# Output projection and FFN of a diffusion block on Trainium2: eight weight slots taken by row tile, and norms per row tile

## What is computed

```python
y = merged @ w_out
h_state = x + g1 * rms_norm(y, norm_mix_post)
h = rms_norm(h_state, norm_ffn_pre) * (1.0 + sc2) + sh2
y = (silu(h @ ffn_w_gate) * (h @ ffn_w_up)) @ ffn_w_down
out = h_state + g2 * rms_norm(y, norm_ffn_post)
```

## Time and profile before

| | us |
|---|---|
| median of 3 runs | 1792.96 |
| lowest, highest | 1792.02, 1793.4 |
| profiled execution | 1793.48 |
| its span | 1791.5 |
| TensorE matmul busy | 1729.5 |
| VectorE busy | 971.5 |
| ScalarE busy | 728.4 |
| POOL busy | 162.8 |

### The profile page before, as it was taken

The page is one execution under the profiler, slowest core; times in us unless marked ns, Lnnn a source line. Parts: engine busy times, 40 slices in busy tenths (PEclk is TensorE's granted clock), DMA queues, the critical chain, the costliest instruction groups (busy, mean ns, idle before and its releaser), DMA issues.

```text
span 1791.5 us, 21671 instructions
## 1 busy us (share of the span) xinstructions
PE 1729.5 (97%) x7916; PEld 1398.9 (78%) x7916; DVE 971.5 (54%) x1036; ACT 728.4 (41%) x798; POOL 162.8 (9%) x178
## 2 busy tenths in 40 slices
PE   4889999999999999999999979999999999999997
PEld 2448888887777888888888868888888888888886
DVE  2326756655675676676565544444444444444444
ACT  3213222215545444554544464444444444343442
POOL 2000000000016552440000000000000000000000
PEclk9999999999999999999999989999999999999999
DMA  8999988987898666565777646666666666766662
GB/s 312 339 361 354 338 317 314 307 282 277 278 338 258 214 188 206 179 195 157 239 228 260 198 136 197 188 192 189 189 188 188 188 189 190 262 190 195 192 194 77
DMA packets 181579, 415.90 MB, mean 232 GB/s; under 512 B 12862, under 2 KB 13150, under 8 KB 171664
## 3 DMA queue, kind: packets, MB, share of 16 engines
q1 hardware_dynamic: 156288, 304.14, 53.9%
q10 hardware_dynamic: 17856, 82.43, 12.7%
q0 software_dynamic: 7376, 28.53, 4.8%
HBM read 394.54 MB, written 20.50 MB: 232 GB/s over the span
## 4 chain that ended last, share of the span: by engine, by line
PE 92%; DMA 2%; ACT 2%; DVE 2%; issue 1%; SPq 0%; POOL 0%; ACTq 0%; DVEq 0%; POOLq 0%
PE ps L1344 28%; PE ps L1348 28%; PE ps L1356 28%; PE ps L1397 1%; DMA raw<-in_w_mod 1%; PE ps L1586 1%; DMA xn<-in_x 1%; PE ps L1602 1%; PE ps L1640 1%; ACT w_hi L594 1%; PE ps L1681 1%; PE ps L1469 0%; PE ps L1557 0%; PE ps L1535 0%; PE ps L1460 0%
## 5 line engine op out<-in xcount | busy, mean ns | idle before, releaser
L935 DVE TENSOR_TENSOR w_lo<-raw,w_hi 128x1024 fp32r<-128x1024 f32 x496 | 612.1, 1237 | 545.9 <-ACT w_hi L594 545.7
L594 ACT ACTIVATE w_hi<-raw 128x1024 fp32r<-128x1024 f32 x496 | 524.8, 1059 | 829.5 <-PE ps L1356 813.5
L1344 PE MATMUL ps<-w_hi,h_hi 128*128 128x512 f32 x1536 | 483.7, 396 | 7.0 <-ACT w_hi L673 7.0
L1348 PE MATMUL ps<-w_hi,h_lo 128*128 128x512 f32 x1536 | 474.1, 390 | 0.0
L1356 PE MATMUL ps<-w_lo,h_hi 128*128 128x512 f32 x1536 | 420.2, 389 | 0.0
L1344 PEld LDWEIGHTS ps<-w_hi,h_hi 128*128 128x128 f32 x1536 | 284.6, 188 | 71.0 <-issue 14.3
L1348 PEld LDWEIGHTS ps<-w_hi,h_lo 128*128 128x128 f32 x1536 | 288.6, 188 | 60.8
L1356 PEld LDWEIGHTS ps<-w_lo,h_hi 128*128 128x128 f32 x1536 | 288.1, 188 | 60.1
L947 DVE SCALAR_TENSOR_TENSOR acc<-wm,csil,acc 128x2048 f32<-128x2048 f32 (+1 forms) x60 | 141.0, 2351 | 97.1 <-DMA wm<-in_w_mod 96.8
L1344 PE MATMUL ps<-w_hi,hid_hi 128*128 128x512 f32 x352 | 108.5, 389 | 0.0
L1348 PE MATMUL ps<-w_hi,hid_lo 128*128 128x512 f32 x352 | 108.3, 389 | 0.0
(11 more groups left out here) (256 smaller groups left out, 1140.7 us busy)
## 6 DMA issues: line engine op xcount, KB each, us to landing
raw<-in_w_in SPq DMA_DIRECT2D x176, 512.0 KB, 5.6
wm<-in_w_mod ACTq DMA_DIRECT2D x64, 1024.0 KB, 7.3
raw<-in_ffn_w_gate SPq DMA_DIRECT2D x88, 512.0 KB, 4.4
raw<-in_ffn_w_up SPq DMA_DIRECT2D x88, 512.0 KB, 4.4
raw<-in_ffn_w_down SPq DMA_DIRECT2D x88, 512.0 KB, 4.7
raw<-in_w_mod SPq DMA_DIRECT2D x64, 512.0 KB, 8.5
raw<-in_w_out SPq DMA_DIRECT2D x32, 512.0 KB, 4.8
px<-stage ACTq DMA_DIRECT2D x44, 256.0 KB, 6.4
```

Of the source, the lines that this page charges most:

```text
L594: act.activation(w_hi[:, j % SPLIT, :, :], raw[:, j % RAW, :, :], ACT.Copy).then_inc(w_high, 1)
L935: dve.tensor_tensor(w_lo[:, j % SPLIT, :, :], raw[:, j % RAW, :, :], w_hi[:, j % SPLIT, :, :].bitcast(F32), ALU.subtract).then_inc(w_low, 1)
L1344: pe.matmul(o, hi[:, kk, c], w_hi[:, q, e, :], start=kk == 0, stop=False)
L1348: pe.matmul(o, lo[:, kk, c], w_hi[:, q, e, :], start=False, stop=False)
```

## The change

The last four slots of the output projection's last block are taken first for row tile 0, then again for row tile 1; so are the first four FFN slots. `UNITS` lists what is turned: eight half units (slot j, one row tile) and four full ones. Everything between the projection and the FFN is done for one row tile at a time: squares, mean, rstd, y times weight, residual (now in four pieces of 512 columns), squares of hs (four pieces). `diag` goes: VectorE writes a normalised copy `hn = hs * rstd` in eight pieces of 512 columns (`HN_ORDER`), and `turn_h2` transposes it with `ident`. The splits of FFN slots 0 to 7 are set between the norms and the units. POOL computes four powers first and then stores both halves of hs. A slot of a by-tile pass signals `w_slot_used` behind tile 1 only.

```diff
+        UNITS = [(j, (m,)) for m in range(MT) for j in range(SPLIT)] + [(j, (0, 1)) for j in range(SPLIT, 8)]
+        HN_ORDER = [(0, 0), (0, 1), (1, 0), (1, 1), (0, 2), (1, 2), (0, 3), (1, 3)]
...
@@ TensorE
+            for m in range(MT):
+                for j in range(8 - SPLIT, 8):
+                    end = S("half_done") if m == 0 and j == 7 else None
+                    products(S_OUT + 8 * (OUT_BLOCKS - 1), j, 2 * j, KT - 1, LAT[m:m + 1], m,
+                             signal=w_used if m == 1 else end)
...
+            def turn_h2(u):
+                j, ms = UNITS[u]
+                pe.wait_ge(S("hn_ready"), max(HN_ORDER.index((m, j // 2)) for m in ms) + 1)
+                if u >= 4:
+                    pe.wait_ge(S("h2_hi_ready"), u - 3)
                 for e in range(2):
-                    for m in range(MT):
-                        last = pe.matmul(bank(4 + j % 4)[:, e * L + m * P:e * L + (m + 1) * P],
-                                         hs[:, m, (2 * j + e) * P:(2 * j + e + 1) * P], diag[:, m, :], start=True, stop=True)
+                    for m in ms:
+                        last = pe.transpose(bank(4 + u % 4)[:, e * L + m * P:e * L + (m + 1) * P],
+                                            hn[:, m, (2 * j + e) * P:(2 * j + e + 1) * P], ident[:, :])
...
+            for u in range(3):
+                turn_h2(u)
+            pe.wait_ge(S("y_scaled"), OUT_BLOCKS - 1)
+            for m in range(MT):
+                for j in range(SPLIT):
+                    pe.wait_ge(S("h2_lo_ready"), SPLIT * m + j + 1)
+                    products(S_FFN, j, 2 * j, KT - 1, LAT[m:m + 1], 2 + m, signal=w_used if m == 1 else None)
+                    if m == 0 and j == 0:
+                        turn_h2(3)
+                    if m == 1:
+                        turn_h2(7 + j)
+                if m == 0:
+                    for u in range(4, 7):
+                        turn_h2(u)
+            for j in range(SPLIT, 8):
+                pe.wait_ge(S("h2_lo_ready"), SPLIT + j + 1)
+                products(S_FFN, j, 2 * j, KT - 1, LAT, 2)
+                if j == SPLIT:
+                    turn_h2(11)
...
@@ ScalarE
+            square_last(0)
+            split(S_FFN, 0)
+            for n in range(OUT_BLOCKS):
+                square_hs(0, n)
+            split(S_FFN, 1)
+            square_last(1)
+            split(S_FFN, 2)
+            take_h2(0)
+            take_h2(1)
+            split(S_FFN, 3)
+            take_h2(2)
+            square_hs(1, 0)
+            take_h2(3)
+            for n in range(1, OUT_BLOCKS):
+                square_hs(1, n)
+            take_h2(4)
+            take_h2(5)
+            for j in range(4, 8):
+                take_h2(j + 2)
                 split(S_FFN, j)
+            take_h2(10)
+            take_h2(11)
...
@@ VectorE
+            mean_squares(0)
+            scale_last(0)
+            for n in range(OUT_BLOCKS):
+                residual(0, n)
+            split(S_FFN, 0)
+            mean_squares_h(0)
+            normal(0)
+            split(S_FFN, 1)
+            mean_squares(1)
+            scale_last(1)
+            low_h2(0)
+            normal(1)
+            split(S_FFN, 2)
+            residual(1, 0)
+            low_h2(1)
+            residual(1, 1)
+            residual(1, 2)
+            low_h2(2)
+            residual(1, 3)
+            split(S_FFN, 3)
+            mean_squares_h(1)
+            low_h2(3)
+            normal(2)
+            normal(3)
+            low_h2(4)
+            low_h2(5)
+            normal(4)
+            normal(5)
+            low_h2(6)
+            normal(6)
+            normal(7)
+            for j in range(4, 8):
+                low_h2(j + 3)
                 split(S_FFN, j)
...
+            low_h2(11)
```

More of the change, by code:

```diff
@@ L151, in build @@
         ssy = keep("ssy", [P, MT, OUT_BLOCKS])
+        ssh = keep("ssh", [P, MT, OUT_BLOCKS])
         stats = keep("stats", [P, 2, MT, 6])
@@ L877, in _, with square_last @@
                     split(S_OUT + 8 * n, j)
-            for j in range(4):
-                split(S_FFN, j)
-            square_y(OUT_BLOCKS - 1, junk, S_FFN, 0)
-            for m in range(MT):
-                act.wait_ge(S("hs_ready"), m + 1)
-                act.wait_ge(S("square"), 4 + m)
-                act.activation(junk[:, :], hs[:, m, :], ACT.Square, accum_out=ssq[:, 2 + m:3 + m]).then_inc(S("square"), 1)
+            def square_last(m):
+                if m == 0:
+                    act.wait_ge(S("half_done"), 1)
+                else:
+                    act.wait_ge(w_used, S_FFN)
+                act.wait_ge(S("y_square"), 2 * OUT_BLOCKS - 2 + m)
+                act.activation(junk[:, 0:N], bank(m), ACT.Square, accum_out=ssy[:, m, OUT_BLOCKS - 1:OUT_BLOCKS])\
+                    .then_inc(S("y_square"), 1)
@@ new lines, in square_hs, with take_h2 @@
+            def square_hs(m, n):
+                act.wait_ge(S("hs_ready"), OUT_BLOCKS * m + n + 1)
+                act.wait_ge(S("square"), 4 + OUT_BLOCKS * m + n)
+                act.activation(junk[:, N:2 * N], hs[:, m, n * N:(n + 1) * N], ACT.Square, accum_out=ssh[:, m, n:n + 1])\
+                    .then_inc(S("square"), 1)
+            def take_h2(u):
+                j, ms = UNITS[u]
+                c = slice(ms[0] * P, (ms[-1] + 1) * P)
+                act.wait_ge(S("h2_turned"), u + 1)
+                if u >= 2:
+                    act.wait_ge(S("h2_lo_ready"), u - 1)
+                for e in range(2):
+                    k = 2 * j + e
+                    act.activation(h2f[:, u % 2, e, c], bank(4 + u % 4)[:, e * L + c.start:e * L + c.stop], ACT.Identity,
+                                   scale=mod2[:, 1, k:k + 1], bias=mod2[:, 0, k:k + 1]).then_inc(S("h2f_ready"), 1)
+                act.wait_ge(S("h2f_ready"), 2 * u + 2)
+                act.activation(h_hi[:, 2 * j:2 * j + 2, c], h2f[:, u % 2, :, c], ACT.Copy).then_inc(S("h2_hi_ready"), 1)
@@ L893, in ffn_block @@
                 for j in range(16):
[L894 to L903, removed]
                     if prev is not None and j == 6:
@@ L911, in ffn_block @@
                             .then_inc(S("silu_ready"), 1)
-                    if prev is not None or j >= 4:
+                    if prev is not None or j >= 8:
                         split(s, j)
@@ L1286, in _, with mean_squares @@
-            dve.wait_ge(S("rstd_ready"), 6)
-            for m in range(MT):
-                dve.tensor_scalar(diag[:, m, :], ident[:, :], rstd[:, 2 + m:3 + m], None, ALU.mult).then_inc(S("diag_ready"), 1)
+            def mean_squares(m):
+                dve.wait_ge(S("y_square"), 2 * OUT_BLOCKS - 1 + m)
+                dve.tensor_reduce(ssq[:, m:m + 1], ssy[:, m, :], AX_X, ALU.add).then_inc(S("ssy_ready"), 1)
+                dve.wait_ge(S("ssy_ready"), 2 * m + 1)
+                dve.tensor_scalar(ssq[:, m:m + 1], ssq[:, m:m + 1], 1.0 / D, EPS, ALU.mult, ALU.add)\
+                    .then_inc(S("ssy_ready"), 1)
@@ new lines, in scale_last, with residual @@
+            def scale_last(m):
+                c = slice((OUT_BLOCKS - 1) * N, OUT_BLOCKS * N)
+                dve.tensor_tensor(y[:, m, c], bank(m), g1w[:, c], ALU.mult).then_inc(S("y_scaled"), 1)
+            def residual(m, n):
+                c = slice(n * N, (n + 1) * N)
+                if n == 0:
+                    dve.wait_ge(S("rstd_ready"), 5 + 2 * m)
+                if n == OUT_BLOCKS - 1:
+                    dve.wait_ge(S("y_scaled"), OUT_BLOCKS + m)
+                dve.scalar_tensor_tensor(out=hs[:, m, c], in0=y[:, m, c], scalar=rstd[:, m:m + 1], in1=hs[:, m, c],
+                                         op0=ALU.mult, op1=ALU.add).then_inc(S("hs_ready"), 1)
@@ L1301, in hidden @@
                                       hid_hi[:, hh, :].bitcast(F32), ALU.subtract).then_inc(S("turned_lo"), 1)
[L1303 to L1309, removed]
+            for j in range(8, 16):
+                split(S_FFN, j)
             with dve.Fori(0, FF_BLOCKS - 1) as i:
@@ L1333, in _, with products @@
         def _(pe):
-            def products(s, j, k, last_k, tiles, first_bank, between=None, used=1):
+            def products(s, j, k, last_k, tiles, first_bank, between=None, used=1, signal=w_used):
                 if isinstance(s, int):
@@ L1356, in products @@
                         last = pe.matmul(o, hi[:, kk, c], w_lo[:, q, e, :], start=False, stop=kk == last_k)
-                last.then_inc(w_used, used)
+                if signal is not None:
+                    last.then_inc(signal, used)
             LAT = [(h_hi, h_lo, 0), (h_hi, h_lo, 1)]
@@ L1689, in ffn_block @@
+            for j in range(SPLIT, 8):
[3 more added lines that the diff above has]
+                    turn_h2(11)
             def ffn_block(s, n, prev):
-                for g in range(2):
+                for g in range(0 if prev is not None else 1, 2):
                     if prev is not None:
```

65 lines of the change are left out of this document (40 added, 25 removed).

## The result

| | before | after |
|---|---|---|
| median, us (7 runs each, same chip) | 1794.28 | 1801.98 |
| lowest to highest | 1792.02 to 1798.33 | 1799.87 to 1803.86 |
| ratio of after to before | | 1.0041 [1.0031, 1.0051] |
| profiled execution, span | 1793.48, 1791.5 | 1802.94, 1801.3 |

The account below looks back on a forecast made before the run. It took TensorE, with 92% of the chain and a 12.3 us wait before the FFN, as the bound. 8.4 less at the full clock minus 1.9 for the clock gave 6.5 less: median 1786.5, range 1785 to 1788.3.

Parts of the forecast that it names:

- 43.52 of products: Sixteen FFN slots after the output projection: 16 x 2.72 us of matmuls, reordered by row tile with nothing added.
- Prices: Instruction costs between projection and FFN: half-unit activation 0.45, scaled piece 0.48, 256-column copy 0.4, subtraction 0.42, POOL power 0.71.
- Waits: TensorE idle: 2.1 and 2.4 before first turns, 1.9 before slot 3 of tile 0, 1.5 before tile 1.
- the sum: From tile 1's start at 1046.3, 40.6 us remain, so slot 15 ends at 1086.9 against 1095.3.
- the walk at the full clock: Engine-by-engine timing from projection to FFN tile 1, before any clock loss; tile 1 starts at 1046.3.
- Clock: Gaps after the projection likely cause one fall of TensorE's clock, costing 1.9 us; bounds nothing to 6.2.
- 8.4 at the full clock: Gain in the projection-to-FFN stretch before clock loss: end at 1086.9 against 1095.3.
- First product: First FFN matmul after the projection: forecast at 1035.7, 11.3 us earlier than before.
- Transposes: Turning in the FFN: 32 calls at 0.109 in place of 0.222 us, 3.6 saved.
- Low clock through the first half: Rival, chance 0.20: turns or waits between half slots keep TensorE slow; 3.4 us less, 1789.6.
- Matmuls that add into one bank: Rival "Slower", chance 0.03: six consecutive half-slot matmuls each wait for the one before; 4 us more, 1797.
- Queues moved past: Later POOL stores of hs, SP loads of FFN slots 8 to 11, and the tail's semaphores cost 0.

Follow-up runs that it names:

- e1: Kernel before plus an unused 32-byte tile that starts the region's tiles 64 bytes later, no instruction changed: 1811.08 against 1793.36, ratio 1.0093.
- e5: Changed kernel with `ssh` in free room behind the region, so every other tile lies where it lay before: 1783.91 against 1793.47, ratio 0.9945.
- e10: e5 with `hn` turned by ordinary float32 matmuls with `ident` in place of transposes: 1788.78, ratio 0.9969.
- experiment 9: Kernel before with normalised copy `hn` for the diagonals, no row-tile order: transposed 1793.28, turned by ordinary matmuls 1793.62; also read the opening's plain transposes in before.
- e15: e5 with only turning units 0 to 2 done by ordinary matmuls, all others by transposes: 1784.82, ratio 0.9947.
- e11: Kernel before with normalised copy `hn`, written in two pieces and transposed, in place of the diagonals, no work by row tile: 1793.28, ratio 0.9998.
- e6: Kernel before with all tiles, weights and activations, 64 bytes further up, distances kept: 1791.56 (one run).
- e12: Kernel before with `hid_lo` alone, stationary in 4 of a down-projection slot's 12 matmuls, 64 bytes further up: 1797.72 (one run).

## Why the prediction was wrong

**The step that failed is one it did not have: the displacement of the tiles.** It priced instructions and waits between 1030.08 and 1095.32, said "Behind 1095.32 nothing of the change acts", and put what the new tile `ssh` does to the rest of the kernel at nothing, without a reason. In the changed stretch its 43.52 of products hold. Outside it 32 new bytes moved the stationary tiles of three stages against their weights, for 8.4 + 2.5 + 7.0 = 17.9. e1 pays 17.7 for the shift alone; e5 is the change without it, 0.55% faster than before.

**The forecast for what it looked at was 6.5 less; 8.1 was measured** in after and e5 alike. Step by step:

*Prices.* Groups of after, 1030 to 1080:

```profile
L911 ACT ACTIVATE h2f<-ps,mod 128x128 f32<-128x128 f32 x16 | 6.4, 447 | 3.5 <-PE ps L1791 3.5
...
L1347 DVE TENSOR_SCALAR hn<-hs,rstd 128x512 f32<-128x512 f32 x8 | 3.6, 483 | 1.1 <-POOL rstd L573 1.1
...
L570 POOL TENSOR_TENSOR rstd<-ssq,minus_half 128x1 f32<-128x1 f32 x2 | 1.1, 554 | 83.7 <-DVE ssq L1315 83.7
```

The half-unit activation came at 0.447 (0.45 taken), the scaled piece at 0.483 (0.48), the copy and subtraction of 256 columns at 0.417 and 0.424 (0.4, 0.42). POOL's power of one column took 0.55 to 0.61 where 0.71, that of two, was taken: 0.1 to 0.15 early at each of four.

*Waits.* 2.1 and 2.4 were forecast before the first turns: 1.9 and 2.3, from the wait rows and the timeline. 1.9 and 1.5 were forecast before slot 3 of tile 0 and slot 0 of tile 1: 2.4 the two together, longest 1.4. Together 6.6, with 8.3 in the sum. These two slots start 12.8 and 16.5 behind the projection's end, where the walk at the full clock had 12.4 and 16.2; from the second on 40.7 pass to the end of slot 15, where the sum had 40.6.

*Clock.* One fall and one stretch at the lower level, as forecast, but the term of 1.9 was too large. From 1045.8 to 1050.5 TensorE's work took twice its time, some 2.3 more. What of it reached the path shows on ScalarE:

```profile
1049.53 0.81 ACT L911 ACTIVATE h2f<-ps,mod 128x128 f32<-128x128 f32 x2 [0.78 <-PE ps L1791]
```

ScalarE waits 0.78 for turn 3, and its last squares, which end TensorE's third wait, come that much later; at the full clock turn 3 would have been there in time. The rest fell into waits for VectorE and ScalarE, whose instructions took no longer. So the clock cost about 0.8, and prices somewhat too high in the walk, POOL's powers above all, gave back about 0.5: the 8.4 at the full clock became 8.1. Of the 1.6 between 6.5 and 8.1, 1.1 is the clock and 0.5 the prices, an estimate from these rows; no run has this order without the fall.

*First product.* 5.6 behind the projection's end was forecast, 5.5 measured.

*Transposes.* 3.6 saved was the sum's share; e10 puts it at 3.1.

*Readings.* "Transposes stand among warm matmuls only, at 1.00" is wrong: those at 24.90 start at 0.50 and bring the clock up (experiment 9). By its own figures the restart of TensorE costs 0.70 - 0.45 = 0.25 and not 0.22, and the clock of before rose 3.4 after work had resumed, not 3.3; neither matters in the sum.

**The rivals.** Low clock through the first half: it did not come, the lower level lasted 6.8. Its mechanism, turns that don't hold the clock up, isn't borne out either: ordinary turns in their place brought no earlier rise (e10, e15), and transposes alone raise it in the opening. Matmuls that add into one bank: the timeline of after, in a half slot of the projection,

```profile
1039.68 0.39 PE L1449 MATMUL ps<-w_hi,h_lo 128*128 128x512 f32 x1
1039.91 0.39 PE L1445 MATMUL ps<-w_hi,h_hi 128*128 128x512 f32 x1
1040.13 0.39 PE L1449 MATMUL ps<-w_hi,h_lo 128*128 128x512 f32 x1
```

has them 0.23 apart, so none waits for the one before. The result lies on the slower side, but not by that rival's mechanism. Queues moved past: no wait in the stretch names a DMA, so 0 stood.

## What to carry to other kernels

When a change adds or removes a tile, list which other tiles it moves, and compare the pitch of matmuls in stages that the change doesn't touch before looking at those that it does. Here the stationary and the moving tile of an fp32r matmul want to lie at a multiple of 256 bytes from each other; place them by explicit offsets, so that a 32-byte accumulator can't move them. A clock fall costs little where the slowed work runs into a wait on another engine anyway (here some 0.8 of 2.3 us), and a saving on TensorE right after a gap can be given back, when the next product waits for another engine and the clock then stays low for longer (e11).

## What was not expected of the hardware

- The pace of a 128x128 by 512 fp32r matmul depends on the distance of its two SBUF operands modulo 256 bytes: 0.2267 us at 0, 0.2333 at 32 and 64, 0.2322 at 128, 0.2289 at 192. 64 bytes further up for all tiles changed nothing (e6), so it isn't the address of one tile. It is worth 17.7 us, 1%, of this kernel. Why, and why 64 and 192 differ, stays open, as does which matmul of a pair pays (e12).
- After the long gap the clock rose 3.2 to 6.1 us after the first ordinary turn (eleven traces), but 9.1 after the first of twelve transposes with a pause of 0.84 behind them (e11, one trace). Yet 32 transposes alone raise it in the opening of all 17 traces, 2.8 to 5.7 after the first. Whether the kind of work or its pauses decide stays open.
- Kernels with before's order differ in the changed stretch by up to 1 us from run to run (73.4 to 74.4), by where the clock falls, and in the opening by about as much. Differences below that in a single run say nothing here.
